# Two output tiles per arriving operand at the four stage starts of a decoder layer on one core

## What is computed

```python
def half_ffn(x, g_pre, wg, wu, wd, g_post):
    n = rmsnorm(x, g_pre)
    return x + 0.5 * rmsnorm((silu(n @ wg) * (n @ wu)) @ wd, g_post)

h = half_ffn(x, ffn1)                       # 1024 -> 2816 -> 1024
parts = rmsnorm(h, g_mix_pre) @ w_in        # queries, keys, values, gates
o = fox_attention(parts), nsa_attention(parts)
h = h + rmsnorm(concat(rmsnorm(o_fox), rmsnorm(o_nsa)) @ w_out, g_mix_post)
y = half_ffn(h, ffn2)
```

## Time and profile before

| | us |
|---|---|
| Median of 3 runs | 1271.16 |
| Lowest and highest run | 1269.64 and 1272.35 |
| The profiled execution's own time | 1269.86 |
| Its span, first to last instruction | 1268.0 |
| TensorE busy with matmuls in the span | 1204.5 |
| VectorE busy | 567.3 |
| ScalarE busy | 450.4 |
| GpSimd busy | 136.5 |

### The profile page before, as it was taken

The page is one execution under the profiler, slowest core; times in us unless marked ns, Lnnn a source line. Parts: engine busy times, 40 slices in busy tenths (PEclk is TensorE's granted clock), DMA queues, the critical chain, the costliest instruction groups (busy, mean ns, idle before and its releaser), DMA issues.

```text
span 1268.0 us, 23847 instructions
## 1 busy us (share of the span) xinstructions
PE 1204.5 (95%) x9643; PEld 1113.6 (88%) x9650; DVE 567.3 (45%) x920; ACT 450.4 (36%) x768; POOL 136.5 (11%) x133
## 2 busy tenths in 40 slices
PE   9999999999999989999899788899999999999995
PEld 6999999999997888789776554797999999999994
DVE  4333332333335674758537642636434332334334
ACT  5232221222344643634435511545223212222332
POOL 0111100001110000312111100020011100010110
PEclk9999999999999999999999899899999999999998
DMA  6222222222123123002706051121222223222221
GB/s 266 100 100 74 77 100 98 90 95 99 63 86 119 53 99 137 2 35 76 236 13 216 20 167 67 56 79 58 76 99 99 74 77 116 100 95 71 73 94 68
DMA packets 46004, 117.97 MB, mean 93 GB/s; under 512 B 4154, under 2 KB 21818, under 8 KB 39874
## 3 DMA queue, kind: packets, MB, share of 16 engines
q1 hardware_dynamic: 42738, 110.95, 25.7%
q10 hardware_dynamic: 3184, 5.88, 1.2%
HBM read 110.93 MB, written 7.97 MB: 94 GB/s over the span
## 4 chain that ended last, share of the span: by engine, by line
PE 85%; DVE 7%; ACT 4%; issue 3%; DMA 1%; ACTq 0%; DVEq 0%; POOL 0%; SPq 0%
PE ps L1319 71%; PE ps L1477 2%; PE ps L1446 2%; PE ps L1461 2%; PE ps L1492 1%; PE ps L1328 1%; PE ps L1611 1%; DVE UT L905 1%; DVE H L909 1%; DVE QST L983 1%; DVE row_max L1070 1%; ACT QST L685 1%; DVE XL L885 1%; PE ps L1620 1%; PE ps L1412 0%
## 5 line engine op out<-in xcount | busy, mean ns | idle before, releaser
L1319 PE MATMUL ps<-XH,WH 128*128 128x260 f32 x1904 | 389.9, 286 | 13.7 <-DVE XL L885 7.4
L1319 PE MATMUL ps<-XH,WL 128*128 128x260 f32 x1904 | 384.1, 283 | 0.0
L1319 PE MATMUL ps<-XL,WH 128*128 128x260 f32 x1904 | 383.4, 283 | 0.0
L407 ACT CAST WH<-RAW 128x1024 fp32r<-128x1024 f32 (+2 forms) x183 | 174.8, 956 | 499.7 <-PE ps L1319 490.7
L1319 PEld LDWEIGHTS ps<-XH,WH 128*128 128x128 f32 x1904 | 295.2, 189 | 21.3 <-DVE XL L885 11.4
L1319 PEld LDWEIGHTS ps<-XH,WL 128*128 128x128 f32 x1904 | 294.0, 189 | 0.0
L1319 PEld LDWEIGHTS ps<-XL,WH 128*128 128x128 f32 x1904 | 293.4, 189 | 0.0
L410 DVE TENSOR_TENSOR WL<-RAW,WH 128x1024 fp32r<-128x1024 f32 (+2 forms) x183 | 203.5, 1112 | 158.2 <-ACT WH L407 156.9
L1319 PE MATMUL ps<-UL,WH 128*128 128x260 f32 x704 | 141.9, 283 | 0.0
L1319 PE MATMUL ps<-UH,WL 128*128 128x260 f32 x704 | 141.5, 282 | 0.0
L1319 PE MATMUL ps<-UH,WH 128*128 128x260 f32 x704 | 141.3, 282 | 0.0
(11 more groups left out here) (232 smaller groups left out, 1013.2 us busy)
## 6 DMA issues: line engine op xcount, KB each, us to landing
RAW<-in_w_gu SPq DMA_DIRECT2D x44, 1024.0 KB, 4.7
RAW<-in_w_down SPq DMA_DIRECT2D x16, 768.0 KB, 4.8
RAW<-in_w_in SPq DMA_DIRECT2D x11, 1024.0 KB, 4.8
RAW<-in_w_down SPq DMA_DIRECT2D x16, 640.0 KB, 4.3
KF<-in_fox_k SPq DMA_DIRECT2D x16, 256.0 KB, 4.6
VF<-in_fox_v SPq DMA_DIRECT2D x16, 256.0 KB, 5.4
RAW<-in_w_out SPq DMA_DIRECT2D x4, 1024.0 KB, 4.8
H<-in_x SPq DMA_DIRECT2D x4, 520.0 KB, 7.1
```

The costliest lines, as they stand in the source:

```text
L407: nc.scalar.copy(WH[:, par, 0:width], RAW[:, slot, j, 0:width]).then_inc(w_hi, 1)
L1319: q = nc.tensor.matmul(ps[:, 2 * slot + half, 0:HALF], w[:, par, cols], x[:, kt0 + kt, half * HALF:(half + 1) * HALF], start=first and kt ...
```

## The change

At all four stage starts the first two output tiles are worked together: for each operand tile, once it has arrived, one step of the first tile and one of the second. Both tiles' weights are needed in step 0 (`ready(k + e)` at `kt == 0`). The first tile signals `items_used` in its last step, the second in its own last step, directly behind.

The squares of operands 0 to 3 are added ahead of the pair's steps 2 to 5. The remaining sum, which raises `hss`, is issued behind the whole pair.

The third output tile goes to slot 3 (banks 6 and 7) in place of slot 0, so that it needn't wait for the evacuation of the first. VectorE reads it from there. Later tiles take slots 0 and 1 in turn as before. In the projections `turn(0)`, which stood behind the second tile, stands behind the third. No instruction is added or taken away; ScalarE's, VectorE's, GpSimd's and SyncE's orders are as before.

```diff
+        def bank_pair(n):
+            return 3 if n == 2 else n % 2
+        def gate_slot(st):
+            return bank_pair(2) if st.kind == "gu" and st.g == 0 and st.number == 1 else 0
...
+            def both_products(k, slots, arrived):
+                for kt in range(KT):
+                    arrived(kt)
+                    cols = slice(kt * P, kt * P + P)
+                    for e in (0, 1):
+                        if kt == 0:
+                            ready(k + e)
+                        for p, (w, x) in enumerate(((WH, XH), (WH, XL), (WL, XH))):
+                            for half in (0, 1):
+                                q = nc.tensor.matmul(ps[:, 2 * slots[e] + half, 0:HALF], w[:, (k + e) % 2, cols],
+                                                     x[:, kt, half * HALF:(half + 1) * HALF],
+                                                     start=kt == 0 and p == 0, stop=kt == KT - 1 and p == 2)
+                        if kt == KT - 1:
+                            q.then_inc(used, 1)
...
             def first_operands(s, kt):
-                if kt >= KT - HSQ_PE:
-                    t = kt - (KT - HSQ_PE)
+                if 2 <= kt < 2 + HSQ_PE:
+                    t = kt - 2
...
-            def token_squares(s, kt):
-                if kt == HSS_AT:
-                    pe.wait_ge(sem("hacc"), since("hacc", s, 1))
-                    all_partitions(Y[:, HSQ_PE, :], 2, start=False).then_inc(sem("hss"), 1)
+            def token_squares(s):
+                pe.wait_ge(sem("hacc"), since("hacc", s, 1))
+                all_partitions(Y[:, HSQ_PE, :], 2, start=False).then_inc(sem("hss"), 1)
...
+                        if known == 0 and st.g == 0:
+                            both_products(k, (0, 1), lambda kt: first_operands(before, kt))
+                            token_squares(before)
+                            return
...
             def project(j0, j1):
-                for j in range(j0, j1):
+                if j0 == 0:
+                    both_products(IT_PROJ, (0, 1), lambda kt: first_operands("a", kt))
+                    token_squares("a")
+                for j in range(j0 or 2, j1):
                     ready(IT_PROJ + j)
-                    if j >= 2:
+                    if j >= 3:
                         pe.wait_ge(sem("projected"), j - 1)
-                    arrived = {0: lambda kt: first_operands("a", kt), 1: lambda kt: token_squares("a", kt)}.get(j)
-                    products((IT_PROJ + j) % 2, KT, XH, XL, j % 2, arrived=arrived)
+                    products((IT_PROJ + j) % 2, KT, XH, XL, bank_pair(j))
+                    if j == 2:
+                        turn(0)
                     if j > j0:
                         turn(j - 1)
...
-            for t in range(KT):
+            both_products(IT_OUT, (0, 1), lambda kt: pe.wait_ge(sem("xlo"), since("xlo", "o", kt + 1)))
+            for t in range(2, KT):
```

More of the change, by code:

```diff
@@ L56 @@
 WARM = (34, 28, 20)
-HSQ_PE, HSS_AT = 4, 2
+HSQ_PE = 4
 DVE_SCALES = 2
@@ L920, in body @@
                         dve.wait_ge(used, k + 1)
-                        nc.vector.tensor_tensor(two(GT[:, st.par, :]), halves(0), two(R1[:, :]),
+                        nc.vector.tensor_tensor(two(GT[:, st.par, :]), halves(gate_slot(st)), two(R1[:, :]),
                                                 ALU.mult).then_inc(sem("evac"), 1)
@@ L1042, in project @@
                                 dve.wait_ge(sem("turned_out"), 1)
-                        nc.vector.tensor_tensor(two(TR[:, j % 4, :]), halves(j % 2), two(R1[:, :]),
+                        nc.vector.tensor_tensor(two(TR[:, j % 4, :]), halves(bank_pair(j)), two(R1[:, :]),
                                                 ALU.mult).then_inc(sem("projected"), 1)
@@ L1233, in _ @@
                 dve.wait_ge(used, IT_OUT + t + 1)
-                nc.vector.tensor_copy(two(Y[:, t, :]), halves(t % 2)).then_inc(sem("ydone_b"), 1)
+                nc.vector.tensor_copy(two(Y[:, t, :]), halves(bank_pair(t))).then_inc(sem("ydone_b"), 1)
                 split(IT_OUT + t + 2)
@@ L1364, in body @@
                     if st.kind == "gu":
-                        first = known == 0 and st.g == 0
+                        if known == 0 and st.g == 0:
+                            both_products(k, (0, 1), lambda kt: first_operands(before, kt))
+                            token_squares(before)
+                            return
                         ready(k)
-                        if not first:
+                        if not gate_slot(st):
                             pe.wait_ge(sem("evac"), since("evac", f, st.M * 2 - (2 if known == 0 else 1)))
-                        products(IT_F[f] % 2, KT, XH, XL, 0,
-                                 arrived=(lambda kt: first_operands(before, kt)) if first else None)
+                        products(IT_F[f] % 2, KT, XH, XL, gate_slot(st))
                         ready(k + 1)
[L1373 to L1376, removed]
+                        pe.wait_ge(sem("evac"), since("evac", f, st.M * 2))
+                        products((IT_F[f] + 1) % 2, KT, XH, XL, 1)
                         return
@@ L1637, in _ @@
             keep_warm(WARM[2], bank=0)
-            for t in range(KT):
+            both_products(IT_OUT, (0, 1), lambda kt: pe.wait_ge(sem("xlo"), since("xlo", "o", kt + 1)))
+            for t in range(2, KT):
                 ready(IT_OUT + t)
-                if t >= 2:
+                if t >= 3:
                     pe.wait_ge(sem("ydone_b"), t - 1)
-                arrived = (lambda kt: pe.wait_ge(sem("xlo"), since("xlo", "o", kt + 1))) if t == 0 else None
-                products((IT_OUT + t) % 2, KT, XH, XL, t % 2, arrived=arrived)
+                products((IT_OUT + t) % 2, KT, XH, XL, bank_pair(t))
             output_squares("b")
```

## The result

The changed kernel takes 1285.75 us (median of four runs, 1285.69 to 1285.84); the kernel before takes 1270.4 on the same count. The ratio is 1.0119, 95% interval 1.0101 to 1.0136: 1.2% slower. The forecast was 1284.0 us.

A forecast was written before the change was run, and what follows sets the result against it. TensorE, with 85% of the chain, was taken as the bound; starts matter only up to the third tile. Later starts of 7.3 us plus 5.6 of clock loss, 12.9 on a median of 1271.16, gave 1284.0 us, range 1277 to 1289.

The forecast's parts named there:

- Third tiles of the second FFN and the projections: Third tile starts: second FFN 0.30 us later, at 881.67; projections at 427.62, as before (427.66); TensorE idles about 4.1 us.
- The gate tile in the projections: Projections: the gate tile's transposes move behind the third tile, so the cast at 438.14 comes at 438.46, +0.32 us.
- The first FFN: First FFN start: TensorE waits from 12.68 to 16.90 for the second tile's low part; third tile at 36.13, +6.34 us.
- The output projection: Output projection start: cast and low part stand open behind the pair; third tile at 818.50 for 818.20, +0.30 us, idle 1.9.
- The clock: Four TensorE idles of about 4 us at stage starts each lower the granted clock: 4 x 1.4 = 5.6 us; output's idle nothing.
- The squares' place: Square sums at the stage starts: the new order of adding them costs nothing by itself, only deciding when the sum is done.
- the one without a clock loss: Rival at the stage starts: TensorE's idles cost only themselves, 1278.5 us; chance 0.10.
- the one without a stall at the first start: Rival in the first FFN: second tile's low part is ready for the second step, 1278.4 us; chance 0.08.
- The rival in which conversion stays hidden: Rival at the four starts: third tile's weights are ready when pair and squares end, 7.0 us won, 1264.2; chance 0.05.
- The rival on banks: Rival in the pairs: going round four PSUM banks brings the clock to 1.2 GHz, 46 us, about 1330; chance 0.02.

## Why the prediction was right, point by point

The direction and the mechanism held, and the size nearly: 12.9 us were forecast, 16.0 came in the profiled span, 15.35 in the medians. That the time itself, 1285.75, lies only 1.75 us above the forecast is in part luck: the median before came out at 1270.4 and not at the 1271.16 that the forecast started from.

- **Third tiles of the second FFN and the projections.** +0.30 and 427.62 forecast; measured +0.31 and -0.04, counted from the start of the stage. TensorE's idle was 3.81 us for the 4.1 forecast. The count from 407.31 in steps of 1.44 and 2.32 us is what the trace shows.
- **The gate tile in the projections.** +0.32 without clock loss; +1.89 measured, of which 1.5 went when the idle was filled. The cast that stood at 438.14 came at 450.56, behind ScalarE's wait of 3.43 us for the turned gate tile, as forecast.
- **The first FFN.** +6.34 forecast, with a stop of 4.2 us after the first step (4.13 measured). Measured 8.48 with the clock; without the 2.1 of slow steps in the pair 6.4.
- **The output projection.** +0.30 forecast; measured +0.51, 0.11 of it ahead of the first matmul of the pair.
- **The clock.** This is the term that was mis-sized: 4 x 1.4 = 5.6 us forecast, 8.4 measured. It is 1.6 (1.59, 1.5, 1.58, 1.59) behind a third tile and 2.1 in the first pair, and there were five falls: the output's idle of 1.85 us, left at nothing, cost 1.6. The row taken for it, 1.7 us behind a gap of 2.25, was the better price than the 1.4 chosen. The reason given for 1.4, that part of the slow time lies in the idle, held only for the first (0.74 in the mean there).
- **Outside the forecast.** 0.5 us from the first weights' landing and -0.4 in the attention between projections and output lie in code that the change doesn't touch.
- **The squares' place.** "Costs nothing by itself" holds, but it hid a gain of 2.9 us in the marks (3.4 in the medians) for the kernel without pairs.

Of the rivals, the one without a clock loss fell by the stretches and by the filled idles, the one without a stall at the first start by the wait of 4.13 us. The rival in which conversion stays hidden set its point at 1.75 us exposed per start; TensorE stood idle for 3.8 us at three and 1.85 at the output, and with the order changed for 1.0 at the three. Even then the kernel stayed 0.2% slower than before, by the losses in the first FFN and at the output. The rival on banks fell: the steps of the pair run at 0.24 us for two matmuls at full clock, and filling the idles gave the clock back with the banks still in turn. The Trainium skill's section "A second HAM failure mode: psum-queue depth-cycling" (TensorE: Matmul & The Clock Gate) describes such a loss; no run here shows one from the banks.

## What to carry to other kernels

A product that is worked on two outputs at once also ends for both at once. Whatever was refilled under the second (here weights with two places) then stands in the open, and so does all that is queued ahead of the refill on its engine: put the refill ahead of any wait for a late result; here that alone took back 11 of the 15 us and made the pair a gain at two of the four starts. And let the second output run ahead only as far as the waits for operands reach: two steps of eight cost nothing at the output, where the full pair lost 2 us. At the second FFN, with the refill in front, both did equally well (24.94 and 24.89 us to the third tile).

## What the runs showed of the hardware

The granted clock is a second price on the idles of TensorE: 1.5 to 1.6 us a time behind the third tiles of the changed kernel, 2.1 in its first pair and 2.6 once in another run (371.53 us for 368.96), and it made 8.4 of 16.0 us. The idle's length alone doesn't decide. The clock fell behind idles of 1.84, 1.85, 2.25 and 3.8 us and once among several of 0.7 to 0.9 us. Of three of 2.4 us in one run it fell behind two, and it stayed full behind those of 0.98 us. Matmuls without use in the idle kept it full at all five places of the one run that had them.

The attention between projections and output, which no edit touched, took from 327.0 to 329.5 us in the profiled runs (327.0 in the changed kernel, 329.0 with the idles filled). A difference of 2 us between two totals of this kernel is for that reason no proof; the marks inside a stage are.
